# Hybrid decoder layer on eight cores: softmax denominators inverted per four heads, convolution ahead of the last attention chunk, first loads re-queued

## Chip, cores and metric

One Trainium2 chip, eight NeuronCores, one program on all of them: each core computes one batch element of eight, and no core talks to another. The metric is the device time in microseconds (us) of the slowest core for one execution.

## What is computed

The reference, cut to what matters here (B = 8, S = 2048, D = 1024, 8 heads of 64):

```python
hn = rmsnorm(x, norm_mix_g);  z = hn @ w_in          # (S, 2560)
a, g, q, k, v = split(z)                             # 512 each
u = a * sigmoid(g)
u = causal_depthwise_conv(u, width=31) + conv_b
conv_out = silu(layernorm(u))
q, k = partial_rope(q), partial_rope(k)              # first 16 dims of a head
# per query: softmax over its own block of 256 keys (causal)
# and over the 3 past blocks whose mean key scores highest
attn = softmax(q @ k.T / 8, selected keys) @ v
h = x + concat(conv_out, attn) @ w_out
h = h + swiglu(rmsnorm(h));  h = h + sigmoid(rmsnorm(h) @ w_gate) * (p @ w_ple)
y = rmsnorm(h)
```

## The kernel before

Everything is kept with channels on the 128 partitions and 512 tokens (a chunk, four in all) on the free axis. Each engine runs its own instruction list in program order; a wait stands in front of the instruction that needs it, so whatever follows on that engine waits too. Waits are worked out by the program from who last wrote or read a buffer.

**Start.** SP issues the loads of the constants `cf` and `cb`, of the positions, and of the first two quarters of x chunk 0; POOL issues the other two quarters and then 16 loads of `w_in` tiles, `wv` and `wtab` (lines 323 to 337; POOL's loads of weights convert f32 to bf16). `rope_tables` (L378) makes sine and cosine with ten DVE instructions (L382 to L393) and four on ACT (L395), writes them to DRAM (`rope_d`) and reads them back spread out as `cs` (L404). Behind it in program order come the squares and the norm of chunk 0 (L371, L374, L346, L362), then `consts` (L870): POOL clears `vs`, `qtz` and small tiles, five MEMSETs of its own.

**Input product and attention.** `win_gen(c)` (L546) makes GLU, q, k, v tiles of chunk c, 20 tiles of eight matmuls (L293), each in a PSUM bank that DVE or ACT empties: GLU by L526 and L530, the rotary tiles by L421 to L426, the rest by ACT copies. `attn_gen(c)` (L590) does the attention of chunk c: 8 heads times 2c+2 units (16, 32, 48, 64 units for c = 0 to 3). A unit is two score matmuls (L605), one ACT exponential of up to 128x1024 (L614) into one of four `pt` slots, on the diagonal a POOL mask (L619), and two matmuls with v (L634). The 64 extra columns of ones in `vs` make the last pair also yield the softmax denominators, 64 equal rows, in the other half of the output bank. At a head's last unit DVE inverts them (L641, RECIPROCAL 64x512 out of PSUM) and multiplies (L642); only then is the bank free. Banks 0 to 3 hold scores, 4 and 5 take turns for outputs, and 6 and 7 serve the dense work.

`interleave` (L303) merges two generators by weights: `win_gen(c+1)` with `attn_gen(c)`. The last attention chunk is merged with `after_conv` (L899 to L907), of total weight 880: `conv_gen` (L690), then output products `wout_gen(0)` and `(1)`, then a norm. During the convolution the attention has bank 4 alone, and the dense work has banks 5, 6 and 7, of which the two sums `bm` and `bs` hold two.

`conv_gen`, 16 channel groups: nine matmuls with diagonal weights that DVE builds (`conv_diag`, L680), a DVE copy out (L697), two ACT instructions (L700, L701), and two matmuls for the LayerNorm sums (L756). Then the statistics on DVE and ACT (L709 to L716), and 16 rounds on POOL (L723, L732), DVE (L727, L738) and ACT (L730), weight 25 each, whose results go through DRAM into `mixc`.

**Rest.** `wout_gen(2)`, `(3)`, the feed-forward net in four weight slices, the gated embedding and the output: PE runs nearly without a gap.

Of the kernel before, what the change touches and what calls it, by code (L numbers as in the profile page):

```python
# [154 lines left out]
def build():  # L155
# [103 lines left out]
    ST, r_st = zip(*[buf("st%d" % i, [128, 4, 512], BF16, 86016 + 4096 * i) for i in range(2)])
    THA, r_tha = zip(*[buf("tha%d" % i, [128, 512], F32, 94208 + 2048 * i) for i in range(2)])  # L260
    CS, r_cs = buf("cs", [128, 2, 512], F32, 98304)
    GATE, r_gate = buf("gate", [128, 4, 8, 8], F32, 102400)
    CMP, r_cmp = buf("cmp", [128, 16, 7, 7], BF16, 103424)
    RANK, r_rank = buf("rank", [128, 16, 8], F32, 104992)
    MBT, r_mbt = buf("mbt", [128, 4, 64], BF16, 105504)
    MASKT, r_maskt = buf("maskt", [64, 512], BF16, 106016)


    KTZ, r_ktz = buf("ktz", [128, 8, T], BF16, 107072)
    QTZ, r_qtz = zip(*[buf("qtz%d" % i, [128, 8, 512], BF16, 139840 + 8192 * i) for i in range(2)])  # L270

    VS, r_vs = buf("vs", [128, 16, 4, 192], BF16, 156224)
    PT, r_pt = zip(*[buf("pt%d" % i, [128, 1024], BF16, 180800 + 2048 * i) for i in range(4)])
    DS, r_ds = zip(*[buf("ds%d" % i, [128, 512], F32, 188992 + 2048 * i) for i in range(2)])
    MIXA, r_mixa_all = buf("mixa", [128, 4, T], BF16, 193088)


    ROP, r_rop = buf("rop", [128, 4, 128], F32, 107072)
    ROT, r_rot = zip(*[buf("rot%d" % i, [128, 256], F32, 107072 + 2048 + 1024 * i) for i in range(4)])
    ROI, r_roi = buf("roi", [128, 256], I32, 107072 + 6144)  # L280
    POSI, r_posi = buf("posi", [128, 128], I32, 107072 + 7168)
    ROW, r_row = buf("row", [128, 128], F32, 107072 + 7680)
# [733 lines left out]
```

How the kernel before makes its waits and increments, by code:

```python
    def wait(self, need):  # L75
        need = {k: n for k, n in need.items() if self.seen.get(k, 0) < n}
        if self.key == "pe":
            need.pop("pe", None)
        for k, n in list(need.items()):
            if any(k2 != k and CLK[(k2, n2)].get(k, 0) >= n for k2, n2 in need.items()):
                del need[k]
        for k, n in need.items():
            self.e.wait_ge(SEMS[k], n)
            for k2, n2 in CLK[(k, n)].items():
                if self.seen.get(k2, 0) < n2:
                    self.seen[k2] = n2
# [1 line left out]
    def mark(self, inst):  # L88
        self.n += 1
        inst.then_inc(self.sem, 1)
        c = dict(self.seen)
        c[self.key] = self.n
        CLK[(self.key, self.n)] = c
        return self.key, self.n
# [106 lines left out]
    def dma(Q, sem, out_ap, in_ap, reads=(), writes=(), parts=()):  # L201
        if sem not in SEMS:
            SEMS[sem] = nc.alloc_semaphore(sem)
            dcnt[sem] = 0
        Q.wait(needs(reads, writes, parts))
        dcnt[sem] += 16
        Q.e.dma_start(out=out_ap, in_=in_ap).then_inc(SEMS[sem], 16)
        t = (sem, dcnt[sem])
        c = dict(Q.seen)
        c[sem] = dcnt[sem]
        CLK[t] = c
        done(t, reads, writes, parts)
        return t
```

## Time and profile before

| | us |
|---|---|
| median of 3 runs (lowest to highest) | 1140.11 (1139.6 to 1141.16) |
| the profiled execution: its time | 1141.19 |
| its span, slowest core (7) | 1139.7 |
| spans of the eight cores | 1130.0 to 1139.7 |
| PE busy, share of the span | 971.1, 85% |
| DVE busy | 614.0, 54% |
| ACT busy | 394.6, 35% |
| POOL busy | 153.7, 13% |

The profile is of core 7. An engine's busy time counts its instructions alone, not its waits. The granted clock of a stretch is the share of full speed at which TensorE ran there; one matmul's own duration overlaps that of the next.

### The profile page before, as it was taken

The page shows a single profiled execution, that of the slowest core. Times are in us where ns is not written, and L with a number is a line of the kernel's source. Part 1 is how long each engine was busy: PE and PEld are TensorE (multiplying, and loading weights), DVE is VectorE, ACT ScalarE, POOL GpSimd, SP SyncE. Part 2 cuts the span into 40 slices and gives each one's busy share as a digit, 9 for nine tenths or more (in the row PEclk, how much of TensorE's full clock was granted, in tenths as well). Part 3 has the DMA queues.
Part 4 walks back from the last instruction along what each step waited for, and adds up shares of the span by engine and source line. Part 5 has one row for each costly group of instructions (what it writes and reads, how often), then busy time and mean ns, then how long its engine had stood idle before and what let it go on. Part 6 is the DMA issues. An engine that isn't in the chain of part 4 may idle for free.

```text
span 1139.7 us, 12651 instructions; the slowest of 8 cores (1130.0 to 1139.7 us)
## 1 busy us (share of the span) xinstructions
PE 971.1 (85%) x4312; PEld 420.3 (37%) x4312; DVE 614.0 (54%) x753; ACT 394.6 (35%) x508; POOL 153.7 (13%) x200
## 2 busy tenths in 40 slices
PE   0876679879868757788999999999999999999785
PEld 0332234334423212233444444444444444444332
DVE  5343686744664445633764444444444444667675
ACT  1342445745634367633431111111111113343543
POOL 7110121101130038402100000100010001000000
PEclk9997899999989876799999999999999999999988
DMA  9953323003340002354980010601060007001103
GB/s 165 183 146 95 81 83 97 16 11 72 86 77 0 1 0 75 96 200 91 166 151 1 1 19 1 120 1 19 1 118 3 1 1 129 1 29 47 74 29 120
DMA packets 49214, 74.23 MB, mean 65 GB/s; under 512 B 11840, under 2 KB 27200, under 8 KB 49024
## 3 DMA queue, kind: packets, MB, share of 16 engines
q0 software_dynamic: 13792, 35.81, 17.2%
q1 hardware_dynamic: 35360, 37.61, 11.8%
q8 instruction: 37, 0.61, 0.2%
q14 instruction: 25, 0.20, 0.1%
HBM read 84.69 MB, written 17.04 MB: 89 GB/s over the span
## 4 chain that ended last, share of the span: by engine, by line
PE 70%; DVE 10%; ACT 7%; DMA 5%; issue 4%; POOL 2%; SPq 2%; DVEq 0%; ACTq 0%; POOLq 0%
PE pd L293 62%; PE pd L605 4%; PE pd L634 4%; DVE ds_76 L641 2%; DMA cs<-rope_d 2%; DVE ds_77 L641 2%; SPq L207 2%; DMA rope_d<-rop 1%; DVE co L697 1%; DMA qk_d<-st_59 1%; DMA posi<-pos 1%; ACT pt_72 L614 1%; ACT pt_73 L614 1%; POOL pt_74 L619 1%; ACT hn_151 L374 1%
## 5 line engine op out<-in xcount | busy, mean ns | idle before, releaser
L806 ACT ACTIVATE thf_171<-pd 128x512 f32<-128x512 f32 x48 | 28.7, 598 | 246.2 <-PE pd L293 234.8
L293 PE MATMUL pd<-ha_56,wa 128*128 128x512 bf16 x256 | 72.6, 424 | 28.5 <-DVE ust L530 13.0
L605 PE MATMUL pd<-qtz_70,ktz 72*128 72x512 bf16 x192 | 62.0, 411 | 27.6 <-ACT pt_72 L614 11.9
L641 DVE RECIPROCAL ds_77<-pd 64x512 f32<-64x512 f32 x16 | 53.6, 3351 | 31.8 <-PE pd L634 31.6
L807 DVE SCALAR_TENSOR_TENSOR t1f_173<-thf_171,pd 128x512 f32<-128x512 f32 x48 | 33.0, 687 | 69.0 <-ACT thf_171 L806 69.0
L641 DVE RECIPROCAL ds_76<-pd 64x512 f32<-64x512 f32 x16 | 53.7, 3359 | 27.8 <-PE pd L634 27.6
L806 ACT ACTIVATE thf_172<-pd 128x512 f32<-128x512 f32 x40 | 23.9, 598 | 105.4 <-PE pd L293 104.5
L807 DVE SCALAR_TENSOR_TENSOR t1f_174<-thf_172,pd 128x512 f32<-128x512 f32 x40 | 27.5, 687 | 60.1 <-ACT thf_172 L806 60.1
L293 PE MATMUL pd<-ha_55,wa 128*128 128x512 bf16 x224 | 53.8, 383 | 6.4 <-DVE ust L530 2.4
L293 PEld LDWEIGHTS pd<-ha_56,wa 128*128 128x128 bf16 x256 | 25.9, 106 | 65.1 <-issue 45.6
L614 ACT ACTIVATE pt_72<-pd 128x1024 bf16<-128x1024 f32 x40 | 40.8, 1020 | 11.4 <-PE pd L605 11.1
L619 POOL TENSOR_TENSOR pt_74<-pt_74,cb_s 128x256 bf16<-128x256 bf16 x24 | 18.6, 775 | 192.3 <-ACT pt_74 L614 191.8
L614 ACT ACTIVATE pt_73<-pd 128x1024 bf16<-128x1024 f32 (+1 forms) x40 | 39.2, 979 | 15.1 <-PE pd L605 15.1
L614 ACT ACTIVATE pt_74<-pd 128x1024 bf16<-128x1024 f32 x40 | 40.9, 1021 | 6.7 <-PE pd L605 6.6
L605 PEld LDWEIGHTS pd<-qtz_70,ktz 72*128 72x128 bf16 x192 | 18.3, 110 | 61.4 <-issue 55.1
L605 PE MATMUL pd<-qtz_69,ktz 72*128 72x512 bf16 (+3 forms) x128 | 34.5, 355 | 6.6 <-DMA ktz<-qk_d 3.2
L293 PE MATMUL pd<-actt_162,wd_169 128*128 128x512 bf16 x176 | 38.6, 379 | 0.0
L293 PE MATMUL pd<-actt_162,wd_161 128*128 128x512 bf16 x176 | 38.6, 379 | 0.0
L293 PE MATMUL pd<-actt_170,wd_161 128*128 128x512 bf16 x176 | 38.6, 379 | 0.0
L293 PE MATMUL pd<-actt_170,wd_169 128*128 128x512 bf16 x176 | 38.6, 379 | 0.0
L614 ACT ACTIVATE pt_75<-pd 128x768 bf16<-128x768 f32 (+1 forms) x40 | 35.7, 893 | 1.9 <-PE pd L605 1.7
L293 PEld LDWEIGHTS pd<-ha_55,wa 128*128 128x128 bf16 x224 | 21.4, 98 | 32.8 <-issue 9.4
(343 smaller groups left out, 1879.0 us busy)
## 6 DMA issues: line engine op xcount, KB each, us to landing
xc<-x POOLq DMA_DIRECT2D x14, 512.0 KB, 12.6
wa<-w_qkc POOLq DMA_DIRECT2D x16, 256.0 KB, 22.5
wd_161<-w_down POOLq DMA_DIRECT2D x11, 256.0 KB, 15.3
wd_169<-w_down POOLq DMA_DIRECT2D x11, 256.0 KB, 15.4
cs<-rope_d SPq DMA_DIRECT2D x16, 128.0 KB
u_d<-ust SPq DMA_DIRECT2D x16, 128.0 KB, 2.7
ktz<-qk_d SPq DMA_DIRECT2D x4, 512.0 KB, 5.3
u_112<-u_d SPq DMA_DIRECT2D x4, 512.0 KB, 9.0
```

What stands on the lines that cost most here:

```text
L207: Q.e.dma_start(out=out_ap, in_=in_ap).then_inc(SEMS[sem], 16)
L293: inst = nc.tensor.matmul(out_ap, l, r, start=(i == 0), stop=(i == n - 1))
L374: op(ACT, lambda: nc.scalar.activation(out=dst[:, k:k + 2, :], in_=src[:, k:k + 2, :], func=AF.Square), reads=rs, writes=[r_dst[k], r_dst[ ...
L605: last = nc.tensor.matmul(dbl[sd][:, j * 512 + of[j]:(j + 1) * 512], KTZ[0:72, h, kt * 128:(kt + 1) * 128], qt[0:72, h, of[j]:512], start= ...
L614: op(ACT, lambda: nc.scalar.activation(out=pt[:, of[0]:1024], in_=dbl[sd][:, of[0]:1024], func=AF.Exp, scale=0.125), reads=[bres[2 * sd], ...
L619: op(POOL, lambda: nc.gpsimd.tensor_tensor(out=dg, in0=dg, in1=trb, op=ALU.mult), reads=[r_cb, r_pt[slot]], writes=[r_pt[slot]])
L634: last = nc.tensor.matmul(bf(ob)[:, of[j]:512], lhs, pt[:, j * 512 + of[j]:(j + 1) * 512], start=(kt == 0), stop=(kt == nkt - 1))
L641: op(DVE, lambda: nc.vector.reciprocal(out=DS[s][num, :], in_=bf(ob)[den, :]), reads=[bres[ob]], writes=[r_ds[s]])
L697: op(DVE, lambda: nc.vector.tensor_scalar(out=CO[:, q, :], in0=bf(b), scalar1=0.5, scalar2=col(C_CB + q), op0=ALU.mult, op1=ALU.add), read ...
L806: op(ACT, lambda: nc.scalar.activation(out=THF[sl][:], in_=bf(bg), func=AF.Tanh, scale=0.5), reads=[bres[bg]], writes=[r_thf[sl]], tab="tanh")
L807: op(DVE, lambda: nc.vector.scalar_tensor_tensor(out=T1F[sl][:], in0=THF[sl][:], scalar=1.0, in1=bf(bg), op0=ALU.add, op1=ALU.mult), reads ...
```

## The change

1. **Denominators.** At a head's end ACT copies the numerators (64x512) to `NUM`, and DVE copies 32 of the denominator rows to `DEN`, which collects four heads on 128 partitions. After the fourth, one RECIPROCAL inverts `DEN`; two DVE instructions split the result into a bf16 value in half the rows and the bf16 remainder (with its sign turned to fit) in the other half; and some units later, per pair of heads, one matmul with a 0/1 matrix `sel` spreads and adds them into the output bank not in use, from which DVE multiplies into `MIXA`.
2. **Order.** The convolution's products and statistics run before the last attention chunk, with banks 0 to 3, 6 and 7. Only the LayerNorm rounds (now `ln_gen`, weight 8 each and 24 after them) and `wout_gen(0)`, `(1)` are merged with the last attention chunk, total weight 312.
3. **Start.** All of x goes through POOL's queue, `cf` and `cb` through ACT's. POOL's MEMSETs in `consts` wait until the rotary tables are made.
4. To make room: three `pt` slots for four, three pairs of `CV` tiles for four, one `RT` buffer for two until `wout_gen(2)`, and most buffers at other addresses.

The core of the diff (buffer addresses left out):

```diff
-    dma(SP, "d_cf", CF[:], cf_h.ap(), writes=[r_cf])
-    dma(SP, "d_cb", CB[:], cb_h.ap(), writes=[r_cb])
+    dma(ACT, "d_cf", CF[:], cf_h.ap(), writes=[r_cf])
+    dma(ACT, "d_cb", CB[:], cb_h.ap(), writes=[r_cb])
...
-            hw = c == 0 and i < 2
-            dma(SP if hw else POOL, "d_x%s%d" % ("h" if hw else "", i), X[:, 2 * i:2 * i + 2, :], ...
+            dma(POOL, "d_x%d" % i, X[:, 2 * i:2 * i + 2, :], ...
...
+    def recip():
+        op(DVE, lambda: nc.vector.reciprocal(out=DEN[:], in_=DEN[:]), writes=[r_den])
+        op(DVE, lambda: nc.vector.tensor_copy(out=RHL[:], in_=DEN[:]), reads=[r_den], writes=[r_rhl])
+        op(DVE, lambda: nc.vector.scalar_tensor_tensor(out=RHL[:], in0=RHL[:], scalar=col(C_LO), in1=DEN[:], op0=ALU.mult, op1=ALU.add),
+           reads=[r_den, r_cf], writes=[r_rhl])
+    def divide(c, pair):
+        b, m = 9 - opools["b"], pair % 4
+        op(PE, lambda: nc.tensor.matmul(bf(b), sel[pair % 2], RHL[:], start=True, stop=True), reads=[r_cb, r_rhl], writes=[bres[b]])
+        op(DVE, lambda: nc.vector.tensor_tensor(out=MIXA[:, pair, c * 512:(c + 1) * 512], in0=NUM[:, m, :], in1=bf(b), op=ALU.mult),
+           reads=[bres[b], r_num[m]], parts=[r_mixa[c]])
...
-                op(DVE, lambda: nc.vector.reciprocal(out=DS[s][num, :], in_=bf(ob)[den, :]), ...
-                op(DVE, lambda: nc.vector.tensor_tensor(out=MIXA[num, h // 2, ...], in0=bf(ob)[num, :], in1=DS[s][num, :], op=ALU.mult), ...
+                op(ACT, lambda: nc.scalar.activation(out=NUM[num, m, :], in_=bf(ob)[num, :], func=AF.Copy), reads=[bres[ob]], ...
+                op(DVE, lambda: nc.vector.tensor_copy(out=DEN[32 * s:32 * s + 32, :], in_=bf(ob)[den, :]), reads=[bres[ob]], ...
+                if s == 3:
+                    recip()
+                    for i in range(2):
+                        due.append((opools["t"] + (4, 7, 8, 8)[c] + 2 * i, lambda i=i: divide(c, h // 4 * 2 + i)))
...
     def consts():
+        POOL.wait(dict([rope_done]))
...
-    set_banks([5, 6, 7])
+    set_banks([0, 1, 2, 3, 6, 7])
...
+    conv = conv_gen()
+    for i in range(4):
+        next(conv)
+    run_due(True)
+    run(conv)
+    set_banks([6, 7])
     def after_conv():
-        yield from conv_gen()
+        yield from ln_gen()
...
-    interleave(after_conv(), 144 + 32 + 3 + 25 * 19 + 90 + 2 * 64 + 8, attn_gen(3), 64, lead=0.05)
+    interleave(after_conv(), 8 * 19 + 24 + 2 * 64 + 8, attn_gen(3), 64, lead=0.05)
...
         run(wout_gen(g))
+        if g == 2:
+            run_due(True)
+            nrt[1] = 2
```

## Rows read from the trace of the kernel before

**Rows 1.** Stretches: start:end, length, busy us of each engine, granted clock, DMA share, GB/s.
```profile
0.00:99.70 99.70, 52.18 (x205) 21.23 (x206) 42.76 (x52) 23.60 (x34) 28.34 (x37) 0.93 0.78 162
99.70:327.30 227.60, 186.71 (x892) 82.54 (x892) 145.96 (x123) 125.76 (x153) 39.20 (x55) 0.93 0.24 59
327.30:406.50 79.20, 57.01 (x217) 21.40 (x218) 35.21 (x33) 27.55 (x43) 4.87 (x9) 0.87 0.16 27
406.50:486.30 79.80, 56.21 (x178) 19.67 (x179) 46.19 (x46) 57.36 (x65) 49.62 (x42) 0.70 0.23 70
486.30:536.40 50.10, 40.97 (x182) 17.59 (x183) 14.92 (x18) 18.38 (x21) 4.86 (x9) 0.97 0.46 130
536.40:1139.70 603.30, 578.03 (x2640) 257.85 (x2640) 328.92 (x482) 141.92 (x195) 26.79 (x50) 0.98 0.25 50
```

**Rows 2.** Chain of waits, first 99.7 us: start, us, what.
```profile
42.37 20.20 DMA cs<-rope_d
...
94.17 5.35 DMA ktz<-qk_d
```

**Rows 3.** Timeline of DVE from 9 us: start, us, line, tiles [idle before, releaser].
```profile
10.46 5.91 DVE L382 CAST row<-posi 128x128 f32<-128x128 int32 x1 [10.46 <-DMA posi<-pos]
16.54 3.45 DVE L383 TENSOR_SCALAR rot_80<-row,cf_s 128x128 f32<-128x128 f32 x1 [0.18 <-DVE row L382]
...
24.65 0.29 DVE L387 CAST rot_82<-roi 128x256 f32<-128x256 int32 x1
...
26.52 0.29 DVE L393 TENSOR_SCALAR rot_83<-rot_83 128x256 f32<-128x256 f32 x1
```

**Rows 4.** Timeline of POOL from 9 us: start, us, line, tiles.
```profile
12.07 0.70 POOL L207 DMA_DIRECT2D wtab_s<-wtab  x1
12.59 3.70 POOL L871 MEMSET vs<- 128x4096 bf16 x1
16.41 3.50 POOL L873 MEMSET qtz_69<- 8x4096 bf16 x1
```

**Rows 5.** DMA issues from 3.0 and from 40.0 us: count, KB, us to landing.
```profile
xc<-x SPq DMA_DIRECT2D x2, 512.0 KB, 14.7
...
xc<-x POOLq DMA_DIRECT2D x1, 512.0 KB, 26.2
```

**Rows 6.** Chain of waits, 99.7 to 327.3 us: shares by line.
```profile
by line: PE pd L293 37.0%; PE pd L605 12.6%; PE pd L634 11.8%; DVE ds_76 L641 7.4%; issue 6.0%; DVE ds_77 L641 4.4%; DVE ust L530 2.4%; ACT pt_72 L614 2.2%; DVE km L448 2.0%; ACT ha_55 L374 1.7%; POOL pt_74 L619 1.4%; ACT vs L543 1.1%; ACT 
```

**Rows 7.** What PE waited for, 99.7 to 327.3 us: total us, times, longest.
```profile
PE pd L293 <- DVE ust L530: 20.3, 8, 7.0
```

**Rows 8.** Lines L641 and L642: count, ns least/median/most, first and last start, shape.
```profile
L641 DVE RECIPROCAL ds_77<-pd x16: 3350/3351/3352, 115.0 to 542.5; 64x512 f32<-64x512 f32 x16
L642 DVE TENSOR_TENSOR mixa<-pd,ds_77 x16: 694/695/695, 118.4 to 546.0; 64x512 bf16<-64x512 f32 x16
```

**Rows 9.** ACT's groups of lines, 0 to 540 us: a copy out of PSUM.
```profile
L419 ACT ACTIVATE st_58<-pd 128x512 bf16<-128x512 f32 x12 | 7.2, 598 | 37.2 <-PE pd L293 37.2
```

**Rows 10.** Timeline of the convolution's first groups.
```profile
331.72 3.68 PE L293 MATMUL pd<-u_112,dg_113 128*128 128x512 bf16 x9 [4.51 <-DVE mixa L642]
335.50 0.75 DVE L697 TENSOR_SCALAR co<-pd,cf_s 128x512 f32<-128x512 f32 x1 [4.04 <-PE pd L293]
336.17 1.35 DVE L680 TENSOR_TENSOR dg_113<-idb,wtab_s 128x1152 bf16<-128x1152 bf16 x1
...
336.40 2.11 PE L293 MATMUL pd<-u_112,dg_114 128*128 128x512 bf16 x9 [1.01 <-DVE co L697]
```

**Rows 11.** First and last of POOL's LayerNorm rounds; score matmuls, 408 to 486 us; exponentials.
```profile
L723 POOL TENSOR_TENSOR tt_126<-co,mean x4: 1261/1263/1515, 408.9 to 454.1; 128x512 f32<-128x512 f32 x4
...
L723 POOL TENSOR_TENSOR tt_129<-co,mean x4: 1262/1262/1264, 419.8 to 466.5; 128x512 f32<-128x512 f32 x4
...
L605 PE MATMUL pd<-qtz_70,ktz 72*128 72x512 bf16 (+2 forms) x87 | 33.8, 480 | 13.8 <-ACT pt_75 L614 7.3 <-ACT pt_72 L614 5.9 <-ACT pt_74 L614 0.4
...
L614 ACT ACTIVATE pt_74<-pd 128x1024 bf16<-128x1024 f32 x40 | 40.9, 1021 | 6.7 <-PE pd L605 6.6
```

More of the change, by code:

```diff
@@ L259, in build @@
[L259 to L266, printed above, removed]
@@ L269, in build @@
[L269 to L278, printed above, removed]
@@ L279, in build @@
[L279 to L282, printed above, removed]
+    sel = [CB[:, 512 + i * 128:640 + i * 128] for i in range(2)]
+    CF, r_cf = buf("cf_s", [128, C_N], F32, 1536)
+    KM, r_km = buf("km", [128, 4, 8], F32, 1952)
+    KMD, r_kmd = buf("kmd", [128, 4, 8, 8], BF16, 2080)
@@ new lines, in build @@
+    HA, r_ha = zip(*[buf("ha%d" % i, [128, 8, 512], BF16, 63488 + 8192 * i, 8) for i in range(2)])
+    UST, r_ust = buf("ust", [128, 4, 4, 128], BF16, 79872, 4)
+    ST, r_st = zip(*[buf("st%d" % i, [128, 4, 512], BF16, 83968 + 4096 * i) for i in range(2)])
+    THA, r_tha = zip(*[buf("tha%d" % i, [128, 512], F32, 92160 + 2048 * i) for i in range(2)])
+    CS, r_cs = buf("cs", [128, 2, 512], F32, 96256)
+    GATE, r_gate = buf("gate", [128, 4, 8, 8], F32, 100352)
+    CMP, r_cmp = buf("cmp", [128, 16, 7, 7], BF16, 101376)
@@ new lines, in build @@
+    RANK, r_rank = buf("rank", [128, 16, 8], F32, 102944)
+    MBT, r_mbt = buf("mbt", [128, 4, 64], BF16, 103456)
+    MASKT, r_maskt = buf("maskt", [64, 512], BF16, 103968)
+    KTZ, r_ktz = buf("ktz", [128, 8, T], BF16, 105024)
+    QTZ, r_qtz = zip(*[buf("qtz%d" % i, [128, 8, 512], BF16, 137792 + 8192 * i) for i in range(2)])
+    VS, r_vs = buf("vs", [128, 16, 4, 192], BF16, 154176)
+    PT, r_pt = zip(*[buf("pt%d" % i, [128, 1024], BF16, 178752 + 2048 * i) for i in range(3)])
+    DEN, r_den = buf("den", [128, 512], F32, 184896)
@@ L285, in mm_gen @@
+    NUM, r_num = buf("num", [128, 4, 512], F32, 186944, 4)
+    MIXA, r_mixa_all = buf("mixa", [128, 4, T], BF16, 195136)
+    ROP, r_rop = buf("rop", [128, 4, 128], F32, 105024)
+    ROT, r_rot = zip(*[buf("rot%d" % i, [128, 256], F32, 105024 + 2048 + 1024 * i) for i in range(4)])
+    ROI, r_roi = buf("roi", [128, 256], I32, 105024 + 6144)
+    POSI, r_posi = buf("posi", [128, 128], I32, 105024 + 7168)
+    ROW, r_row = buf("row", [128, 128], F32, 105024 + 7680)
     def mm_gen(out_ap, pairs, reads, b, piece=4, preads=None):
@@ L585, in win_gen, with run_due @@
         yield from nxt
-    opools = {"o": [4, 5], "n": 0}
+    opools = {"b": 4, "t": 0}
+    due = []
+    def recip():
[8 more added lines that the diff above has]
+           reads=[bres[b], r_num[m]], parts=[r_mixa[c]])
+    def run_due(all=False):
+        while due and (all or due[0][0] <= opools["t"]):
+            due.pop(0)[1]()
+            if all:
+                opools["b"] = 9 - opools["b"]
     def attn_gen(c):
@@ L699, in conv_gen @@
             bank_put(b)
[L700 to L701 removed]
+            op(ACT, lambda: nc.scalar.activation(out=CV1[q % 3][:], in_=CO[:, q, :], func=AF.Copy), reads=[r_co[q]], writes=[r_cv1[q % 3]])
+            op(ACT, lambda: nc.scalar.activation(out=CV2[q % 3][:], in_=CO[:, q, :], func=AF.Square), reads=[r_co[q]], writes=[r_cv2[q % 3]])
             if q + 4 < 16:
@@ L952, in _consts @@
     cb[:, 384:512] = np.kron(np.eye(4), np.ones((32, 32))) / 512.0
+    for i in range(4):
+        for r in (0, 16):
+            cb[32 * i + r, 512 + 64 * i:576 + 64 * i] = 1.0
     blk = (np.arange(T)[None, :] // 256 == np.arange(8)[:, None]).astype(np.float32)
```

125 lines of the change are left out of this document (59 added, 66 removed).

## The prediction

> **What bounds the kernel now.** I read the stretches first, then the chain of waits in each stretch, then what PE waited for there, and the timelines where a wait is disputed. In the stretches [rows 1] the reader should see two kernels. From 536.4 us to the end PE is busy 578.0 of 603.3 us at a granted clock of 0.98: TensorE is the bound, the change issues the same instructions there, and I leave that part as it is (2640 matmuls, so 0.229 us for each, stops included). Before it PE is the bound nowhere for long: 186.7 of 227.6 us at 0.93 while chunks 1 to 3 go through the input product, 57.0 of 79.2 in the convolution, 56.2 of 79.8 at a clock of 0.70 in the LayerNorm rounds. All that can be won lies in these first 536 us.
>
> In the first 99.7 us the chain never touches PE: it goes from the positions through the rotary tables to `rope_d`, `cs` and `ktz` [rows 2]. Its first part is odd [rows 3]: a CAST of 128x128 takes 5.91 us where one of 128x256 takes 0.29 a little later, and L383 takes 3.45 us. The POOL timeline says why [rows 4]: POOL's DMA issues run to 12.77 us, then two MEMSETs of 3.70 and 3.50 us, and CAST and L383 end just when a MEMSET does. (L384 beside the third, likewise.)
>
> From 99.7 to 327.3 us the two RECIPROCAL groups hold 7.4 + 4.4 = 11.8% of the chain, 26.9 us [rows 6], and PE's largest single wait is for `ust`, 20.3 us in 8 waits [rows 7], a GLU product that stands in DVE's list behind a RECIPROCAL. The convolution shows its own limit [rows 10]: its first group waits 4.51 us for the last head's bank, the next starts 1.01 us after PE ran dry, when L697 has emptied the only bank left to it.
>
> **The start.** Removed: the MEMSETs from beside the tables. CAST, L383 and L384 (3.5 like L383) then cost some 0.3 each as L387 does, 0.9 for 12.9 us. Against it, the CAST starts later: it got nothing done from 10.46 to 12.59 us, when only DMA issues stood on POOL, and two more x loads at 0.70 us each [rows 4] move their end from 12.8 to 14.2. Tables ready at 26.8 before (L393), then at about 14.2 + 0.9 + 0.3 of gaps + 3.1 (the unchanged rest, from 23.7 on, where the third MEMSET and L384 end) = 18.5: **8 us less**. Bounds: nothing; and 12 if the CAST isn't held and x alone decides (x quarters on SP landed 14.7 us after issue, at about 18 [rows 5]; ahead of the weights on POOL's queue I put them at 13 to 14). `cf` and `cb` on ACT cost two issues before ACT has work. The MEMSETs, 11.3 us in all, then run from about 19.5 to 31 in front of POOL's x loads for chunk 1, which wait for the norm anyway; and on their queue they stand behind the weights, so that their landing (40 + 26.2 = 66 us [rows 5]) hardly moves. That is a floor under chunk 1's norm, but not under `cs` and `ktz`, which shift with the tables and end the stretch [rows 2]. I take 8 at 99.7 us.
>
> **Denominators.** Per four heads, before: 4 x (3.35 + 0.69) = 16.2 us of DVE [rows 8]. After: four copies, two splits and two multiplies at 0.69 each (L642, the nearest row; for copies and splits an upper end), and one RECIPROCAL: 8 x 0.69 + 3.4 = 8.9 us. The price of a RECIPROCAL of 128 partitions out of SBUF is not shown; nearest is L641, 64 partitions out of PSUM, 3.35 us, which I take; bounds 1.7 (twice as fast out of SBUF) and 6.7 (partitions counting). Eight groups: 58 us less DVE work. On the chain only what PE waited for counts: of 24 RECIPROCALs in the middle 6 remain, three quarters of 26.9 us go, 20. Added: 12 spreading matmuls (of 16) at 0.23, 2.7 us of PE; 24 ACT copies at 0.60 [rows 9] beside 125.8 busy of 227.6, off the path, in the worst case all on it, 14. The clock rises with fewer stops: 186.7 busy us at 0.93 hold at most 13 us of that; I take a quarter, 3. Sum: **20 us less**, bounds 6 (20 - 14) and 35 (the 26.9 whole, and most of the clock). Next in line is what remains of the `ust` wait behind norms and copies, then the exponentials. Each new wait: ACT's copy waits for a head's last output matmul, with the next exponential behind it, which PE then misses for about a matmul pair; the spreading matmul waits for the split result, but comes 4 to 8 units after it. Three `pt` slots instead of four: an exponential waits for the output matmuls of three units before, which PE has passed two units ago; nothing. One `RT` buffer: norms are a chunk apart; nothing, at worst one norm's eight L362, 5.4 us.
>
> **Convolution alone.** 16 groups of 11 matmuls, 176 x 0.225 = 39.6 us, plus 1.6 for a slow first group (3.68 against 2.11 [rows 10]) and 1.5 for the two spreading matmuls behind the last RECIPROCAL: 43 us, and it starts without the 4.51 us wait, since banks 6 and 7 and the score banks are free. DVE needs 0.75 + 1.35 = 2.1 us per group [rows 10], under PE's 2.5. Before, 79.2 us: 36 less. But 13 units of attention ran beside it (26 of 128 score matmuls) and now come later.
>
> **LayerNorm rounds with attention.** By the weights 35 units now fall here, before 43.5 (87 score matmuls [rows 11]) in 79.8 us. POOL was busy 49.6 us there for 16 rounds [rows 1], 3.1 each; the rounds took (466.5 - 408.9)/15 = 3.84 [rows 11]. I take POOL's 3.1 as the new pace, 50 us, since the five RECIPROCALs that stopped PE there shrink to one or two; plus 4.5 for the statistics ahead of them (six instructions, L709 to L716, an estimate from 0.69 each), and 5 units behind the rounds at ACT's pace, 57.4/43.5 = 1.32 each (the exponential's 1.02 [rows 11] and its share of the rest), 7: 61.5, **18 less**. Bounds: 51 (4.5 and all 35 units at ACT's pace) and 75 (4.5, rounds at today's 3.84, 5 units at today's 79.8/43.5 = 1.83).
>
> **Output products with attention.** 29 units and 128 matmuls in place of 8 and 128: 28.8 + 29.4 x 4 x 0.225 x 0.9 (diagonal units are shorter) 23.8 + 1.8 for the norm's sums + 1.6 stops = 56 against 50.1: **6 more**; PE is dense there, at 0.97 [rows 1].
>
> **Sum.** -8 - 20 - 36 - 18 + 6 = -76. The profiled execution took 1141.2 (span 1139.7), 1.1 above the median, so I expect 1065 by its measure and **1064** as a median.
>
> **One rule against the trace.** L383 beside a MEMSET took 3.45 us [rows 3, 4]; no row has a two-input DVE instruction beside a MEMSET, and after the change the squares and norms of chunk 0 are just that. The Trainium skill (SBUF — State Buffer, "Who interferes with whom") says that such an instruction is blocked by a GpSimd one that reads SBUF, not by one that only writes it; by that rule the 8 us stay. By the price of L383 they go, the first rival.
>
> **The rivals.**
> (a) The MEMSETs, 11.3 us, hold DVE's squares and norms as they held L383: the start gains 8 - 11 = -3, time 1075. For it: three instructions held. Against: all three have one input.
> (b) Attention without matmuls beside it stays at the lower clock. For it: 0.70 in today's rounds [rows 1]. A unit's matmuls then take 4 x 0.45 x 0.9 = 1.62 us, with today's idle PE time (79.8 - 56.2)/43.5 = 0.54 on top 2.16, 35 units 76 in place of 57: 1083. The Trainium skill (TensorE: Matmul & The Clock Gate, Part 1) says that the clock is halved by default and activity releases it; the 0.70 agrees.
> (c) RECIPROCALs were hidden, and other DVE work takes their place: the middle gains 5, time 1079. Against: 11.8% of the chain.
> (d) ACT's copies stand before the exponentials on the path: 32 x 1.2 (0.60 and a wait as long) = 38, time 1102.
> (e) Slower: the clock falls to half from the convolution to the end of the output products, since the dense convolution no longer fills attention's gaps. Price 40 (convolution) + 19 (as in b) + 52 (output products) = 111, time 1175; it decides once 76 of it is lost, 68%. Against: the same matmuls run at 0.97 in today's output products.
> That the change doesn't do what it says I see only as (c).
>
> **Chances.** Forecast (1034 to 1090 without a rival) 0.58; (a) 0.10; (b) 0.14; (c) 0.07; (d) 0.06; (e) and other losses 0.05. A measurement of this kernel tells 0.2%, 2.3 us. Only (e) and its like are slower, 0.04, with 0.01 within. The range takes the forecast's bounds together with (a) to (c): 1034 (every term at its best, 12 + 35 + 36 + 29 - 6 = 106 less) to 1097 (close to the worst, 0 + 6 + 36 + 5 - 6 = 41 less); outside lie (d), (e) and the forecast's tails.
>
> **What would show it.** Tables ready (L393's end) at 18 to 19 us, not 26.8; L383 under 0.5; first score matmul at 90 to 92. Eight RECIPROCALs of 3.4 us, `ust` waits under 8 us. Convolution 40 to 45 us at a clock near 1. POOL's rounds 3.1 us apart. PE's last dense stretch still 603 us long. The prediction is wrong if that stretch changes, if one of DVE's squares (L371) takes over 2 us, if rounds keep 3.8, or if exponentials wait behind the copies.

## The result, and the profile after

The changed kernel is faster, by a third of what was forecast: 1113.3 us, and 1115.6 in the profiled execution (span 1114.0), against 1140.1; the ratio is 0.9774, 95% interval 0.975 to 0.9798. (Two more executions, in which the four cores of one half of the chip showed a lower clock, are left out.) The forecast was 1064, range 1034 to 1097.

The stretches of the changed kernel, columns as in [rows 1], core 3; the sixth is new, output products 2 and 3:

```profile
0.00:100.66 100.66, 57.90 (x205) 21.50 (x206) 33.59 (x52) 24.19 (x34) 29.87 (x39) 0.83 0.80 161
100.66:319.70 219.04, 188.17 (x901) 82.59 (x902) 100.65 (x125) 137.70 (x176) 42.93 (x54) 0.95 0.25 61
319.70:363.93 44.23, 40.79 (x180) 17.56 (x178) 33.34 (x34) 19.11 (x34) 4.01 (x8) 0.96 0.31 48
363.93:435.03 71.10, 48.08 (x144) 15.80 (x144) 34.83 (x41) 50.77 (x60) 50.41 (x40) 0.69 0.25 74
435.03:502.56 67.53, 56.53 (x254) 24.45 (x254) 16.35 (x24) 37.02 (x41) 5.66 (x9) 0.95 0.26 85
502.56:539.47 36.91, 33.35 (x148) 14.62 (x147) 27.14 (x38) 11.41 (x14) 7.07 (x14) 0.95 0.89 174
539.47:1114.00 574.53, 549.12 (x2505) 244.71 (x2503) 304.56 (x448) 131.89 (x185) 21.61 (x41) 0.98 0.21 44
```

Cut at the same events in both traces (first score matmul, chunk 2's last product with v, last matmul of the convolution's statistics, first output product, first of group 2, first feed-forward matmul), they give the account that the rest of this text explains:

| stretch | before | changed | forecast | measured |
|---|---|---|---|---|
| start | 99.7 | 100.7 | -8 | +1.0 |
| middle | 227.2 | 219.0 | -20 | -8.2 |
| convolution | 79.6 | 44.2 | -36 | -35.4 |
| LayerNorm rounds | 79.8 | 71.1 | -18 | -8.7 |
| output products 0, 1 | 47.8 | 67.5 | +6 | +19.8 |
| output products 2, 3 | 31.8 | 36.9 | 0 | +5.1 |
| rest | 573.8 | 574.5 | 0 | +0.7 |
| sum | 1139.7 | 1114.0 | -76 | -25.7 |

One term came as worked out. The other five missed by 5 to 14 us each, all on the same side.

**The start.** DVE's timeline answers to [rows 3]; the rows at 14.11, 17.92 and 23.22 us ran beside POOL's MEMSETs (14.13 to 25.9 us), and the last is the first product with `cs`:

```profile
5.99 0.34 DVE L384 CAST row<-posi 128x128 f32<-128x128 int32 x1 [5.99 <-DMA posi<-pos]
6.50 0.35 DVE L385 TENSOR_SCALAR rot_80<-row,cf_s 128x128 f32<-128x128 f32 x1 [0.18 <-DVE row L384]
...
10.61 0.29 DVE L395 TENSOR_SCALAR rot_83<-rot_83 128x256 f32<-128x256 f32 x1
...
14.11 1.23 DVE L373 TENSOR_TENSOR ha_56<-xc 128x1024 bf16<-128x1024 f32 x1 [2.07 <-DMA xc<-x]
...
17.92 5.39 DVE L364 SCALAR_TENSOR_TENSOR ha_56<-xc,cf_s,rt_49 128x512 bf16<-128x512 f32 x8 [2.59 <-ACT rt_49 L349]
23.22 2.94 DVE L905 COPY idb<-cb_s 32x32 bf16<-32x32 bf16 x4
...
49.58 0.69 DVE L424 TENSOR_TENSOR tha_61<-pd,cs 128x512 f32<-128x512 f32 x1 [13.98 <-DMA cs<-rope_d]
```

The tables end at 10.9 us, 16 earlier than before and better than the 18.5 forecast, and `cs` has landed by 49.6, 13 earlier than before (42.37 + 20.20 = 62.6 [rows 2]); but the first score matmul comes at 100.7. SP's timeline shows where the gain ends; below it are pieces of the chain, as in [rows 2]:

```profile
11.99 0.40 SPq L207 DMA_DIRECT2D rope_d<-rop  x1
24.30 2.67 SPq L207 DMA_DIRECT2D cs<-rope_d  x4
...
28.89 31.78 SPq L207 DMA_DIRECT2D u_d<-ust  x4
60.83 7.14 SPq L207 DMA_DIRECT2D qk_d<-st_59  x5
72.18 0.64 SPq L207 DMA_DIRECT2D qtz_70<-qk_d  x1
```
```profile
32.23 17.08 SPq L207
...
49.39 11.28 SPq L207
...
82.85 12.20 DMA qk_d<-st_60
95.10 5.42 DMA ktz<-qk_d
```

SP takes 31.8 us over the four GLU writes (two issues alone take 17.1 and 11.3), so the query tiles' first write leaves at 60.8 us, and their read-back follows only at 72.2. Until 60 us the DMA engines are nearly full; their busy tenths over the first 80 us, 2 us each:

```profile
DMA  0798999999999999989999998999946555531898
```

**The middle.** What PE waited for, as in [rows 7]: the wait for GLU products fell from 20.3 to 7.6, and the waits for exponentials rose to 7.8 in sum (5.0 before).

```profile
PE pd L296 <- DVE ust L533: 7.6, 6, 3.7
...
PE pd L627 <- ACT pt_73 L636: 3.3, 5, 0.9
...
PE pd L627 <- ACT pt_75 L636: 2.7, 3, 1.3
...
PE pd L627 <- ACT pt_74 L636: 1.8, 4, 0.8
```

### The profile page after: what moved, and what is told of

It reads as the page before. It is cut to its first block, busy times and chain, and to the rows that moved or that the text cites. A ratio compares the mean times of both kernels' runs of the same rounds, so it can differ in the third digit from the quotient of the medians.

```text
span 1114.0 us, 12760 instructions; the slowest of 8 cores (1108.7 to 1114.0 us)
## 1 busy us (share of the span) xinstructions
PE 973.9 (87%) x4328; PEld 421.2 (38%) x4328; DVE 550.5 (49%) x761; ACT 412.1 (37%) x540; POOL 161.6 (15%) x202
## 4 chain that ended last, share of the span: by engine, by line
PE 72%; ACT 7%; DVE 6%; SPq 4%; issue 4%; POOL 3%; DMA 3%; DVEq 0%; ACTq 0%; POOLq 0%
PE pd L296 62%; PE pd L627 5%; SPq L207 4%; PE pd L655 4%; DMA wa<-w_qkc 1%; DVE den L596 1%; ACT pt_73 L636 1%; DMA qk_d<-st_60 1%; POOL pt_73 L641 1%; PE pd L510 1%; ACT pt_74 L636 1%; ACT pt_75 L636 1%; ACT hn_149 L376 1%; POOL yh_130 L758 1%; ACT hn_150 L376 1%
## 5 line engine op out<-in xcount | busy, mean ns | idle before, releaser
L664 DVE COPY den<-pd 32x512 f32<-32x512 f32 x32 | 21.9, 684 | 74.2 <-PE pd L655 73.8
L636 ACT ACTIVATE pt_73<-pd 128x1024 bf16<-128x1024 f32 (+1 forms) x54 | 53.3, 987 | 14.1 <-PE pd L627 13.9
L636 ACT ACTIVATE pt_74<-pd 128x1024 bf16<-128x1024 f32 (+1 forms) x53 | 52.1, 984 | 5.1 <-PE pd L627 5.0
L636 ACT ACTIVATE pt_75<-pd 128x1024 bf16<-128x1024 f32 (+1 forms) x53 | 50.8, 958 | 3.6 <-PE pd L627 3.5
L655 PE MATMUL pd<-pt_73,vs 128*128 128x512 bf16 (+1 forms) x108 | 34.4, 404 | 8.0 <-POOL pt_73 L641 8.0
L655 PE MATMUL pd<-pt_74,vs 128*128 128x512 bf16 (+1 forms) x106 | 32.3, 391 | 6.3 <-POOL pt_74 L641 6.3
L662 ACT ACTIVATE num<-pd 64x512 f32<-64x512 f32 x32 | 18.9, 591 | 47.9 <-PE pd L655 47.8
```

The lines of the kernel that those rows point to most:

```text
L636: op(ACT, lambda: nc.scalar.activation(out=pt[:, of[0]:1024], in_=dbl[sd][:, of[0]:1024], func=AF.Exp, scale=0.125), reads=[bres[2 * sd], ...
L655: last = nc.tensor.matmul(bf(ob)[:, of[j]:512], lhs, pt[:, j * 512 + of[j]:(j + 1) * 512], start=(kt == 0), stop=(kt == nkt - 1))
L662: op(ACT, lambda: nc.scalar.activation(out=NUM[num, m, :], in_=bf(ob)[num, :], func=AF.Copy), reads=[bres[ob]], **({"writes": [r_num[m]]} ...
L664: op(DVE, lambda: nc.vector.tensor_copy(out=DEN[32 * s:32 * s + 32, :], in_=bf(ob)[den, :]), reads=[bres[ob]], **({"writes": [r_den]} if s ...
```

## The experiments

Each is the changed kernel with the edit shown. Stretches in us as above; times are ratios to the kernel before, with intervals; the profile of each is of its slowest core unless a core is named, and a median is that of its eight cores.

| run | start | middle | conv. | LayerNorm | out 0, 1 | out 2, 3 | ratio (95%) |
|---|---|---|---|---|---|---|---|
| changed | 100.7 | 219.0 | 44.2 | 71.1 | 67.5 | 36.9 | 0.9774 (0.975 to 0.9798) |
| e1 old start | 98.1 | 219.1 | 44.1 | 71.7 | 67.6 | 36.9 | 0.9771 (0.9733 to 0.9809) |
| e2 GLU writes later | 94.2 | 219.0 | 44.2 | 71.1 | 65.9 | 38.0 | 0.973 (0.9701 to 0.9759) |
| e3 old division | 99.7 | 228.8 | 42.2 | 76.0 | 72.8 | 32.1 | 0.9907 (0.9881 to 0.9932) |
| e4 squares on DVE | 100.0 | 219.1 | 44.2 | 71.1 | 52.6 | 38.1 | 0.9661 (0.9643 to 0.9679) |
| e5 norm later | 99.2 | 219.0 | 44.2 | 71.1 | 66.0 | 37.4 | 0.9771 (0.9755 to 0.9787) |
| e6 subtractions on DVE | 98.3 | 218.5 | 44.2 | 59.8 | 67.6 | 36.9 | 0.969 (0.9674 to 0.9706) |
| e7 filling matmuls | 99.8 | 219.5 | 44.1 | 71.6 | 67.6 | 36.9 | 0.9796 (0.9781 to 0.9812) |
| e8 numerators on DVE | 98.4 | 218.8 | 45.6 | 71.1 | 67.6 | 38.5 | 0.9797 (0.9772 to 0.9821) |
| e9 three together | 99.3 | 219.1 | 44.2 | 58.4 | 52.6 | 32.6 | 0.9517 (0.9502 to 0.9532) |
| e10 q, k first (core 6) | 93.6 | 219.1 | 44.2 | 71.1 | 65.9 | 37.9 | 0.9725 (0.9709 to 0.9742) |
| e11 all | 94.2 | 218.2 | 44.2 | 59.7 | 52.6 | 32.6 | 0.9455 (0.9439 to 0.9471) |
| e12 no RECIPROCAL | 100.1 | 214.6 | 42.1 | 70.6 | 65.8 | 32.6 | 0.9684 (0.9666 to 0.9702) |
| e13 k's writes ahead | 98.2 | 216.1 | 44.2 | 71.1 | 65.9 | 38.1 | 0.9713 (0.9689 to 0.9738) |
| e14 all, k ahead | 97.5 | 215.7 | 44.2 | 58.7 | 52.6 | 32.6 | 0.9442 (0.9422 to 0.9461) |
| e15 that, old start (core 2) | 97.6 | 216.6 | 44.1 | 58.4 | 52.6 | 32.6 | 0.954 (0.9482 to 0.9598) |
| e16 e14, chunk 1's x late | 102.4 | 215.4 | 44.2 | 59.8 | 52.6 | 32.6 | 0.9522 (0.947 to 0.9574) |

### The division: e3, e12, e8

e3 puts `before`'s L641 and L642 in the place of the numerator and denominator copies, `recip` and `divide`:

```diff
-                op(ACT, lambda: nc.scalar.activation(out=NUM[num, m, :], in_=bf(ob)[num, :], func=AF.Copy), ...
...
+                op(DVE, lambda: nc.vector.reciprocal(out=DS[s][num, :], in_=bf(ob)[den, :]), ...
+                op(DVE, lambda: nc.vector.tensor_tensor(out=MIXA[num, h // 2, ...], in0=bf(ob)[num, :], in1=DS[s][num, :], op=ALU.mult), ...
```

> The old division (RECIPROCAL and product of each head by itself), with the changed order and start. Theory (the grouped denominators gave the middle its 8 us and keep the last chunk's attention from stops): the stretch from the first score matmul to chunk 2's last output product takes 226 to 230 us in place of 219.0, PE's wait for the GLU products is 18 to 22 us again in place of 7.6, the rest is 5 to 15 longer, the time 1126 to 1138. Rival (the RECIPROCALs were hidden behind other work, and the 8 us come from elsewhere): the middle 217 to 221, the time 1112 to 1118.

The middle took 228.8 us, and PE waited for the GLU products as before the change:

```profile
PE pd L297 <- DVE ust L534: 19.9, 8, 7.0
```

So the new division is worth 9.8 us in the middle on the slowest cores (7.6 by the medians, 226.4 and 218.8), 5 in the rounds and 5 in the output products, and costs 2 in the convolution and 5 at the end (32.1 became 36.9). The rival falls. The same run against the kernel before tells what order and start are worth without the division: some 11 us of the 26.

e12 leaves the inversion out (a copy stands in its place):

```diff
-        op(DVE, lambda: nc.vector.reciprocal(out=DEN[:], in_=DEN[:]), writes=[r_den])
+        op(DVE, lambda: nc.vector.tensor_copy(out=DEN[:], in_=DEN[:]), writes=[r_den])
```

> The changed kernel with each RECIPROCAL replaced by a copy of the same tile (the inversion is left out). It tells what the eight that are left still cost. Theory (they stand mostly beside other work, so that a third of their 20 us in the middle is on the path): the middle 212 to 216 us in place of 219.0, the time 1104 to 1110. Rival (the wait for the GLU products and the chain's other DVE pieces have other causes): the middle 217 to 220, time 1110 to 1115.

The middle is 214.6, 4.4 shorter: the theory. With e3, all 24 RECIPROCALs were worth 9.8 + 4.4 = 14 us there (11 by the medians, 226.4 and 215.1), not the 26.9 that stand on the chain [rows 6]. What PE waits for then shows who takes over, the exponentials, 5.2 us in e3:

```profile
PE pd L627 <- ACT pt L636: 9.6, 12, 2.2
...
PE pd L296 <- DVE ust L533: 4.7, 6, 1.3
```

e8 moves the numerators:

```diff
-                op(ACT, lambda: nc.scalar.activation(out=NUM[num, m, :], in_=bf(ob)[num, :], func=AF.Copy), ...
+                op(DVE, lambda: nc.vector.tensor_copy(out=NUM[num, m, :], in_=bf(ob)[num, :]), ...
```

> The 32 copies of numerators on VectorE in place of ScalarE. Theory (the copies cost little on ScalarE, which isn't the bound of the middle, and something in the last chunk's attention): the middle 217 to 223 us, LayerNorm rounds and output products together 1 to 6 shorter than 175.5, the time 1108 to 1116. Rival (d) of the prediction (the copies stand ahead of exponentials that PE waits for, 32 x 1.2 us): 15 to 38 us less, time 1076 to 1099.

On the slowest core no stretch got clearly shorter but the start, which differs by 2 to 3 us from core to core; the time, 1116.0 to 1117.4, is at the upper end of the theory's range and above it. Rival (d) falls: nothing like its 38 us was on the path. That core ran the middle at a granted clock of 0.94, though, and the other seven needed 213.2 to 217.8 us there, against 218.2 to 219.4 in the changed kernel; so the copies may cost some 3 us in the middle, which the convolution (1.4 longer) and the end (1.6 longer) partly took back.

### The LayerNorm rounds: e6, e7

```diff
-                op(POOL, lambda: nc.gpsimd.tensor_tensor(out=TT[s][:], in0=CO[:, q, :], in1=MEAN[:], op=ALU.subtract),
+                op(DVE, lambda: nc.vector.tensor_tensor(out=TT[s][:], in0=CO[:, q, :], in1=MEAN[:], op=ALU.subtract),
```

> The changed kernel, with the 16 subtractions of the mean (1.26 us each) on VectorE in place of GpSimd. Theory (GpSimd, 50.4 us busy of 71.1, sets the pace of the LayerNorm rounds and makes the diagonal masks late): from the last statistics matmul to the first output product 56 to 65 us in place of 71.1, the time 1102 to 1109. Rival (b) of the prediction (PE at its lower clock sets the pace): 69 to 73 us, time 1112 to 1116.

e7 adds matmuls of constants into a free bank, three ahead of each half round (`yield 8` became twice `yield 4`):

```diff
+            last = nc.tensor.matmul(bf(6), bones, CB[:, 0:512], start=True, stop=True)
```

> The changed kernel with 114 matmuls added that nobody reads (three ahead of each half of a LayerNorm round, constants times constants, 24 us of PE at full speed), to keep PE denser. Theory (GpSimd sets the pace of the rounds): the granted clock of that stretch rises from 0.69 to over 0.85, its length stays at 69 to 76 us. Rival (b) of the prediction (PE at its lower clock sets the pace): the clock rises and the stretch takes 56 to 65 us in spite of the added work, time 1099 to 1109.

The stretch in both, e6 first:

```profile
360.97:420.72 59.75, 42.69 (x143) 14.22 (x144) 40.95 (x57) 50.42 (x60) 31.05 (x24) 0.77 0.31 94
```
```profile
363.40:434.98 71.58, 61.09 (x257) 25.04 (x258) 35.20 (x41) 50.78 (x60) 50.19 (x40) 0.90 0.23 71
```

With the fill the clock rises from 0.69 to 0.90 and the stretch stays, 71.6 against 71.1: the low clock follows from PE's waiting and doesn't set the length. With 16 subtractions off POOL (50.4 us busy, now 31.1) it is 59.8, and the clock rises by itself. POOL sets the pace, and rival (b) falls. In e6 ACT is the next, 50.4 busy of 59.8. The Trainium skill (TensorE: Matmul & The Clock Gate, Part 1) has the clock follow PE's activity; e7 agrees.

### The output products beside attention: e4

```diff
-                square2(H[g], r_h[g], 1, HN[g], r_hn[g], d - 1)
+                square2(H[g], r_h[g], 1, HN[g], r_hn[g], d - 1, dve=g < 2)
```

> The changed kernel, with the squares of the output products of groups 0 and 1 (eight of them, beside chunk 3's attention) on VectorE in place of ScalarE. Theory (on ScalarE each stands waiting for two sums, with the next exponential queued behind it, and PE misses that): the stretch from the first output product to the last of group 1 takes 56 to 62 us in place of 67.5, the time is 1103 to 1110. Rival (that stretch goes at the exponentials' own pace or at PE's clock): 66 to 69 us, time 1112 to 1116.

The changed kernel's timeline shows the cause, ACT's rows first and then PE's:

```profile
459.17 1.06 ACT L376 ACTIVATE hn_149<-h_145 128x1024 bf16<-128x1024 f32 x1 [5.73 <-DVE h_145 L811]
460.13 1.01 ACT L636 ACTIVATE pt_73<-pd 128x1024 bf16<-128x1024 f32 x1
```
```profile
458.97 0.59 PE L655 MATMUL pd<-pt_75,vs 128*128 128x512 bf16 x2
461.28 0.33 PE L627 MATMUL pd<-qtz_71,ktz 72*128 72x256 bf16 x2 [1.71 <-ACT pt_73 L636]
```

ACT idles 5.73 us in front of a square whose two sums aren't there yet; the exponential behind it, whose scores are, starts only at 460.13, and PE stops for it. With the squares on DVE:

```profile
434.31:486.87 52.56, 52.39 (x253) 23.95 (x253) 26.18 (x32) 30.17 (x33) 5.89 (x9) 1.00 0.33 112
```

PE hardly stops (0.2 us), and its clock is full. Of the 15.0 us, 9.8 were PE's waits for exponentials (4.0 + 3.8 + 2.0), 1.1 one for a mask, and 4.1 the same matmuls at a clock of 0.95 instead of 1.00 (56.5 busy us against 52.4). The theory holds, and was too modest.

### The end of the last attention chunk: e5, e9

e5 takes group 0's norm behind `run_due`:

```diff
-        yield from norm_gen(H[0], r_h[0], 1, 1, HN[0], r_hn[0], squares=False)
...
+            run(norm_gen(H[0], r_h[0], 1, 1, HN[0], r_hn[0], squares=False))
             nrt[1] = 2
```

> The changed kernel, with group 0's norm behind the last division and group 2's output products instead of ahead of them. Theory (the norm's eight products and the last RECIPROCAL stand on VectorE ahead of group 2's sums, and PE runs out of banks): from group 2's first output product to the first FFN matmul 32 to 35 us in place of 36.9, though the norm's sums now lie in it, and 2 less before it; time 1108 to 1112. Rival (PE's stop there comes from the last division itself): no less than 36 us, time 1112 to 1116.

37.4 us on the slowest core, where the theory fails; the other seven took 34.3 to 35.9, against 35.2 to 38.1 in the changed kernel, and the time, 1112.3 to 1114.5, hardly moved. In the changed kernel PE stops like this; the first row is PE's wait in front of the spreading matmul (L603), the others DVE's list up to group 2's sums (L811), the last of which it waits for:

```profile
PE pd L603 <- DVE h_147 L811: 3.6, 1, 3.6
```
```profile
504.21 5.39 DVE L364 SCALAR_TENSOR_TENSOR hn_149<-h_145,cf_s,rt_49 128x512 bf16<-128x512 f32 x8 [4.68 <-ACT rt_49 L349]
509.63 0.68 DVE L664 COPY den<-pd 32x512 f32<-32x512 f32 x1
510.42 3.35 DVE L596 RECIPROCAL den<-den 128x512 f32<-128x512 f32 x1
...
515.08 4.87 DVE L811 TENSOR_TENSOR h_147<-pd,h_147 128x512 f32<-128x512 f32 x8
```

In e5 that wait is 0.9. But the norm's sums (8 matmuls) had filled PE's wait for the last mask; without them PE came out of a gap, and on the slowest core the stretch began at half the clock:

```profile
499.46:503.46 4.00, 3.78 (x11) 1.48 (x11) 3.58 (x2) 0.59 (x1) 3.37 (x8) 0.50 0.88 155
503.46:507.46 4.00, 4.00 (x16) 1.57 (x14) 2.92 (x5) 0.66 (x1) 2.70 (x5) 0.79 0.98 180
```

So e9 leaves the sums where they are and moves only DVE's eight products, with the edits of e4 and e6:

```diff
-        yield from norm_gen(H[0], r_h[0], 1, 1, HN[0], r_hn[0], squares=False)
+        yield from rms_bank(HN[0], r_hn[0], b)
+        rt0.append(rms_rt(b))
...
             run_due(True)
+            scale0()
```

> The squares on VectorE and the subtractions on VectorE together, and group 0's norm cut in two: its sums stay where they are, so that PE has no gap there, and its eight products on VectorE come behind the last division. Theory (three separate queues, so the gains add): LayerNorm stretch 58 to 61 us, output products of groups 0 and 1 52 to 54, from there to the first FFN matmul 32 to 35, time 1083 to 1089. Rival (the freed time is taken by ScalarE, 50 us busy in the shorter LayerNorm stretch, or the parts overlap): 1090 to 1102.

All three came: 58.4, 52.6, 32.6 us, 1083.9 to 1085.7 in all. e12 had 32.6 too: without the RECIPROCAL's 3.35 us the sums come earlier as well. But norm and RECIPROCAL stood in front of group 2's sums before the change, too ([rows 8], 542.5 us), and PE hardly stopped (0.5 us); nor does it for a sum in e3, with the old division in the new order, where these are all its waits behind the last attention chunk:

```profile
PE pd L656 <- POOL pt L642: 1.1, 1, 1.1
PE pd L297 <- DVE mixa L664: 0.9, 1, 0.9
```

So the new part is the spreading matmul. It needs one particular bank, the output bank not in use, which one of group 2's tiles has taken by then, and it waits until the last of the eight sums is done (515.08 + 4.87 us). The two edits shorten that wait by bringing the sums forward.

### The start: e1, e2, e10, e11, e13 to e16

e1 takes back the start:

```diff
-    dma(ACT, "d_cf", CF[:], cf_h.ap(), writes=[r_cf])
+    dma(SP, "d_cf", CF[:], cf_h.ap(), writes=[r_cf])
...
+            hw = c == 0 and i < 2
...
-        POOL.wait(dict([rope_done]))
```

> The start as in the kernel before (cf, cb and half of x's chunk 0 on SP, no wait ahead of the MEMSETs), all else changed. Theory (the first stretch ends with what SP's queue and the DMA engines have left to do, not with the tables): the tables are ready at about 27 us again, the first score matmul stays at 99 to 103, the time at 1112 to 1118. Rival (the tables set the end of the stretch, and the change lost what they gave elsewhere in it): the first score matmul 16 us later than in the changed kernel, at 115 to 118, the time at 1128 to 1132.

98.1 us (98.6 by the median of the eight cores, 99.4 in the changed kernel), and the same time: what the change does to the start is worth nothing in the changed kernel. e2 issues chunk 0's GLU writes behind its query and key tiles:

```diff
+        if c == 0:
+            for i in range(4):
+                store_u(0, i)
```

> The changed kernel, with the four writes of chunk 0's GLU products to memory issued on SP behind the query and key tiles' way through memory instead of ahead of it. Theory (SP stands 31.8 us in those four issues and holds the query tiles' writes behind them): the query tiles' first write is issued by 55 us in place of 60.8, the first score matmul comes at 82 to 92, the time is 1098 to 1108. Rival (the DMA engines have the same bytes to move until about 66 us whatever is issued first): the first score matmul at 98 to 102, time within 3 us of 1114.

94.2 (median 91.5), and 4 to 7 us in the time: between the two. The queries' writes left at 51.1 us in place of 60.8, and landed at 69.4 in place of 72.2. e10 goes further, weights 8 to 15 first and `qk()` ahead of the GLU tiles:

```diff
-    for i in range(16):
+    for i in list(range(8, 16)) + list(range(8)):
...
-        if c in (1, 2):
+        if c < 3:
             yield from qk()
```

> The changed kernel, with chunk 0's query and key tiles ahead of its GLU tiles, and their weights (the second half of the 16 tiles) loaded first: the way of queries and keys through memory then lies beside the GLU and value tiles, and SP issues it ahead of the GLU products. Theory (the order on SP's queue and the weights' order set the first score matmul): it comes at 72 to 86 us, the time is 1088 to 1102. Rival (as long as the DMA engines are full, until about 66 us, those transfers take as much longer): the first score matmul at 90 to 100, time 1104 to 1114.

The rival: 93.6. Of six executions four took 1108.5 to 1110.1 us and two 1114.8 and 1118.3; in the profiled one (1114.8) cores 0 and 1 needed 6 to 11 us more in the middle than the others, so core 6 is shown. SP's timeline there:

```profile
49.45 3.08 SPq L207 DMA_DIRECT2D qk_d<-st  x5
69.52 0.66 SPq L207 DMA_DIRECT2D qtz<-qk_d  x1
70.28 2.61 SPq L207 DMA_DIRECT2D cs<-rope_d  x4
73.05 3.52 SPq L207 DMA_DIRECT2D qk_d<-st  x5
...
88.43 2.82 SPq L207 DMA_DIRECT2D u_d<-ust  x4
```

SP waits until 69.5 with the queries' read-back for their write to land, and the keys' writes stand behind it. e11 is e10 with e9's edits.

> The two before it together: query and key tiles first, squares and subtractions on VectorE, the norm cut in two. Theory (all four are separate places of the path): the time is the changed kernel's less the sum of the two gains, between 1058 and 1076. Rival (a later start of other transfers, or a stage that is then short of ScalarE): 1077 to 1090.

1077.6 to 1078.1: the rival, by a hair; the gains of e9 (29) and e10 (5 to 6) do add, but e10's was smaller than its theory.

e13 is e10 with the keys' writes issued ahead of that read-back, e14 adds e9's edits, e15 is e14 with the old start:

```diff
+                if c == 0 and which == 1:
+                    qk_read(0, 0)
+                    qk_read(0, 1)
+                    load_cs(1)
```

> As with the query and key tiles first, and for chunk 0 the key tiles' writes to memory issued ahead of the query tiles' read-back, which waits 17 us on SP for the queries' writes to land; chunk 1's part of the tables is read after both. Theory (SP's order: four trips through memory stand one behind the other): the first score matmul at 74 to 85 us, time 1092 to 1103. Rival (the DMA engines are full until about 66 us and set it): 88 to 95 us, time 1104 to 1112.

> That, with squares and subtractions on VectorE and the norm cut in two. Theory (separate places of the path): 29 us less than without them, time 1063 to 1074. Rival (the earlier start is given back by chunk 1's input, which lands no earlier): 1075 to 1081.

> The same with the start of the kernel before (cf, cb and half of x's chunk 0 on SP, no wait ahead of the MEMSETs), so that the tables are ready at about 27 us again. Theory (with SP's order out of the way the tables begin the chain that sets the first score matmul): it comes 8 to 16 us later than in the run before, the time is 6 to 16 us longer. Rival (the DMA engines hide it still): within 3 us of it, in both.

In time e13 and e14 went the rivals' way: nothing is gained over e10 and e11. But the theory was right about the keys: their read-back leaves at 72.5 us in e13 and 71.1 in e14, in place of 87.7 in e10. The first score matmul is even later, 98.2 in e13, because chunk 1's part of `cs`, now read last, holds chunk 1's first query tile for 7.3 us, and that stands ahead of it on PE. An order in which both come early wasn't run. e15 lies between: by the medians the start is 98.8 us against 94.2 in e14, so 4.6 of the tables' 14 to 16 us come through once SP's order is out of the way (one execution each, and in e14 the cores lie between 87.3 and 97.5). Its time, 1081.2 to 1094.5, is 4 us longer where only that counts; in the profiled run two cores lost another 10 us in the middle, which stays open. SP's timelines in e14 and e15 (core 2):

```profile
49.02 11.74 SPq L207 DMA_DIRECT2D qk_d<-st  x10
68.42 0.66 SPq L207 DMA_DIRECT2D qtz<-qk_d  x1
71.14 0.60 SPq L207 DMA_DIRECT2D ktz<-qk_d  x1
```
```profile
62.25 6.43 SPq L207 DMA_DIRECT2D qk_d<-st  x10
68.79 0.67 SPq L207 DMA_DIRECT2D qtz<-qk_d  x1
```

Issued from 49 or from 62 us, the queries' writes have landed at 68.4 and 68.8, when their read-back leaves. e16 takes chunk 1's x (2 MB) out of that time:

```diff
+                    POOL.wait(needs([r_qd[1][0]], []))
+                    load_x(1)
```

> As the kernel with all four gains and the key tiles' writes ahead, but chunk 1's x (2 MB, 12 us at the 165 GB/s of that stretch) is loaded only when the key tiles' writes have landed. Theory (the DMA engines' other work sets when the query tiles' writes land): they have landed, and the read-back is issued, at 54 to 62 us in place of 68.4; chunk 1's norm comes later for it, so the time is 1070 to 1086. Rival (their own form, rows of 1 KB, or SP sets it): 66 to 70 us.

```profile
47.98 9.85 SPq L207 DMA_DIRECT2D qk_d<-st  x10
61.87 0.66 SPq L207 DMA_DIRECT2D qtz<-qk_d  x1
```

They land 6.5 us earlier, at the edge of what the theory expected; chunk 1's x, then loaded from 65.1 us, makes its norm late, the first score matmul comes at 102.4, and the time is 1081.7 to 1083.7 (1092.8 in one of four executions). So up to the landing of the queries' writes the start is the DMA engines', and what e16 took out of their queue was missed a few us later. The 24 to 29 us from there to the first score matmul (40 in e16) are trips through memory and chunk 1's first tiles; how short they could be isn't shown.

## Why the prediction was right or wrong

1. **Convolution, -36: right** (-35.4), with its terms: 176 matmuls at a clock of 0.96, no first wait. Attention not run beside it came back later, as forecast.
2. **The start, -8: wrong.** The step that failed: "That is a floor under chunk 1's norm, but not under `cs` and `ktz`, which shift with the tables". The tables came even earlier, and `cs` did shift with them, by 13 us; `ktz` did not. Between the two stand the queries' writes. In the changed kernel SP's GLU writes hold them until 60.8 us and they have landed at 72.2, as before (71.6); but issued at 49.0, 51.1 or 62.3 us (e14, e2, e15) they have landed only at 68.4, 69.4 and 68.8. I took a chain of DMA waits for latencies that shift; this one was a queue that empties at about a fixed time. e1 shows that the tables no longer count, e16 that the queue does (2 MB less, 6.5 us earlier), and e15 that 4.6 us would come through if SP's order weren't in the way as well. Rival (a) fell: the squares and the norm beside MEMSETs took 1.23 and 5.39 us (8 x 0.67), as without them (before, 1.22 and 5.4). The Trainium skill's rule (SBUF — State Buffer, "Who interferes with whom") holds here.
3. **The middle, -20: right in kind, mis-sized.** "three quarters of 26.9 us go, 20": it was 9.8 (e3; 7.6 by the medians), and all 24 RECIPROCALs were worth 14 (11). The chain gives a RECIPROCAL its full length wherever it ended last, but without it PE stops for the next in line. PE's own wait, 20.3 [rows 7], was the better bound: 12.7 of it went, and the waits for exponentials, 7.8 in place of 5.0, took about 3 back. The RECIPROCAL's price (3.35 for 128 partitions out of SBUF) was as taken.
4. **LayerNorm rounds, -18: right cause, wrong sum.** POOL is the pace: 16 rounds from 366.4 us, the last beginning at 416.0, are 3.31 each against the 3.1 taken, 3 us. The larger miss is "5 units behind the rounds at ACT's pace, 57.4/43.5 = 1.32 each": of the stretch's 74 score matmuls 48 ran beside the rounds and 22 behind them, 11 units in 15.7 us (1.43 each). Weights fix the order of PE's list, not the time at which POOL gets through its rounds.
5. **Output products 0 and 1, +6: wrong**, +19.8. "PE is dense there, at 0.97": with 8 units it was, with 29 it wasn't. I listed "ACT's copy ... with the next exponential behind it" as a new wait, but not the squares, which stood on ACT in the same place all along and had few exponentials behind them. With them away it is 52.6 us, 4.8 more than before: the sum of matmuls was right.
6. **Output products 2 and 3, 0: wrong**, +5.1. The step is "the change issues the same instructions there, and I leave that part as it is". It doesn't: the last division, which fell into that part before as well, now ends in a spreading matmul, and this waits 3.6 us for a bank that one of group 2's tiles holds, until the last of eight sums; behind the stop the clock falls to 0.81 and 0.76 for 8 us. With the old division there (e3) it is 32.1.

Of the rivals none came as a whole: (a), (b) and (d) fell in the runs named; (c) came nearest, since the middle gained 8.2 between its 5 and the forecast's 20; for (e) the clock stayed at 0.96 in the convolution and 0.95 in the output products.

So the -76 left out three waits (items 2, 5 and 6: 9, 14 and 5 us) and took two terms at twice their worth (items 3 and 4: 12 and 9 us).

## What to carry to other kernels

A change that moves much work next to other work has to be priced queue by queue: list what already stands on each engine in the new neighbourhood and waits for something late, not only what the change adds. A share of the chain of waits was about twice the gain here; the waits of the engine that matters, less what is next in line, came closer. In a stretch full of transfers, issuing one earlier gained little here, and moving one out of it was paid back where its data was needed.
